# A four-layer decoder trunk with expert retrieval: wide weight pieces in the second layer, per-head waits, three value slots on VectorE while mixing, and a shorter second mixing

## The reference

```python
def peer(xn, w_q, sub_keys, u_tab, v_tab):
    q = (xt @ w_q).reshape(t, PEER_HEADS, 2, PEER_HALF)          # 8 heads
    s = einsum("thpd,hpnd->thpn", q, sub_keys)
    ...                                                           # top 16 of each half, top 16 of the 256 sums
    idx = take_along_axis(cand_idx, pos, axis=-1)                 # 128 experts per token
    g = softmax(top_s, axis=-1)
    ...
        u = take(u_tab, ic, axis=0)                               # (128 tokens, 8, 16, 1024)
        a = einsum("cd,chkd->chk", xc, u)
        w = gc * gelu(a)
        vv = take(v_tab, ic, axis=0)
        return einsum("chk,chkd->cd", w, vv)
```

## Time and profile before

| | |
|---|---|
| runs of the kernel | 1623.74, 1624.48, 1624.27 us; median 1624.27 us |
| profiled execution | 1625.22 us, of which the span of instructions is 1623.3 us |
| PE, DVE, ACT, POOL busy | 1339.6, 1073.2, 468.5, 1013.6 us |
| DMA | 617.13 MB, mean 380 GB/s |
| gathers (q0), weights and the rest (q1) | 536.94 MB, 79.26 MB |
| granted TensorE clock, mean | 0.91 |

### The profile page before, as it was taken

How to read it: one execution, slowest core, us unless ns; L and a number is a source line. 1 busy time by engine, 2 the same in 40 slices (tenths; PEclk the granted TensorE clock), 3 DMA queues, 4 the chain that set the end, 5 groups by cost and what they waited for, 6 DMA issues and landing times.

```text
span 1623.3 us, 17094 instructions
## 1 busy us (share of the span) xinstructions
PE 1339.6 (83%) x4558; PEld 769.0 (47%) x4558; DVE 1073.2 (66%) x2529; ACT 468.5 (29%) x1427; POOL 1013.6 (62%) x1099
## 2 busy tenths in 40 slices
PE   7999798888895899888777799989877978777775
PEld 7887544444552564354343376546444433322222
DVE  4248689988775545637787635664877977755555
ACT  0203333333332222432233221441333322211112
POOL 0006677777547655766666745675777677777774
PEclk9999999999997998899989899999988989888887
DMA  9519999999999999999999999999999999999997
GB/s 335 180 57 369 397 396 409 404 405 405 393 389 365 399 391 394 407 406 390 400 402 403 410 392 387 402 392 367 408 401 404 409 410 409 409 409 409 410 409 274
DMA packets 222153, 617.13 MB, mean 380 GB/s; under 512 B 18881, under 2 KB 88571, under 8 KB 222075
## 3 DMA queue, kind: packets, MB, share of 16 engines
q0 software_dynamic: 147456, 536.94, 84.0%
q1 hardware_dynamic: 74619, 79.26, 14.7%
HBM read 615.07 MB, written 1.05 MB: 380 GB/s over the span
## 4 chain that ended last, share of the span: by engine, by line
PE 33%; DMA 20%; POOL 15%; issue 13%; DVE 11%; ACT 6%; POOLq 0%; SPq 0%; DVEq 0%; ACTq 0%
DMA u_ring<-in_peer_u_dram,idx_now 18%; PE acc L807 16%; PE tile L777 13%; POOL v_ring L532 8%; POOL u_ring L532 7%; DVE u_ring L1022 5%; ACT diag L622 2%; ACT gelus L616 2%; DMA v_ring<-in_peer_v_dram,idx_now 2%; PE tile L909 1%; PE xf L777 1%; PE tile L904 1%; DVE xres L1049 0%; ACT pq L718 0%; PE tile L799 0%
## 5 line engine op out<-in xcount | busy, mean ns | idle before, releaser
L807 PE MATMUL acc<-v_ring,diag 128*128 128x512 f32 x1780 | 864.7, 644 | 117.7 <-ACT diag L622 64.8
L1022 DVE CUSTOM_DVE_ANT_0 u_ring<-u_ring,xf 128x1024 f32<-128x1024 f32 x512 | 613.5, 1215 | 275.3 <-DMA u_ring<-in_peer_u_dram,idx_now 273.0
L532 POOL DMA_INDIRECT v_ring<-in_peer_v_dram,idx_now x512 | 497.1, 971 | 291.8 <-PE acc L807 119.8
L807 PEld LDWEIGHTS acc<-v_ring,diag 128*128 128x128 f32 x1780 | 363.0, 209 | 589.3 <-issue 550.6
L532 POOL DMA_INDIRECT u_ring<-in_peer_u_dram,idx_now x512 | 501.2, 979 | 168.7 <-issue 138.9
L608 ACT ACTIVATE gelus<-dots 128x8 f32<-128x8 f32 x64 | 13.4, 209 | 526.4 <-DVE dots L1022 526.4
L622 ACT ACTIVATE diag<-ident,gelus 128x128 f32<-128x128 f32 x448 | 137.8, 388 | 2.1
L777 PE MATMUL tile<-w_ring,fT 128*128 128x256 f32 x480 | 110.3, 383 | 3.7 <-DVE fT L1171 3.7
L777 PEld LDWEIGHTS tile<-w_ring,fT 128*128 128x128 f32 x480 | 92.1, 193 | 27.4 <-issue 12.0
L616 ACT ACTIVATE gelus<-gelus,gates 128x1 f32<-128x1 f32 x512 | 102.1, 281 | 4.1 <-ACT gelus L608 2.3
L726 ACT ACTIVATE gexp<-best,gstat 128x16 f32<-128x16 f32 x32 | 9.8, 307 | 308.3 <-DVE best L1312 308.3
(11 more groups left out here) (170 smaller groups left out, 1046.1 us busy)
## 6 DMA issues: line engine op xcount, KB each, us to landing
w_ring<-in_peer_wq_dram SPq DMA_DIRECT2D x21, 1024.0 KB, 16.4
w_ring<-in_w_out_dram SPq DMA_DIRECT2D x12, 1024.0 KB, 24.0
w_ring<-in_w_kv_dram SPq DMA_DIRECT2D x12, 1024.0 KB, 16.5
u_ring<-in_peer_u_dram,idx_now POOLq DMA_INDIRECT x512, 10.7
v_ring<-in_peer_v_dram,idx_now POOLq DMA_INDIRECT x512, 10.6
w_ring<-in_w_in_b_dram SPq DMA_DIRECT2D x8, 1024.0 KB, 20.8
u_ring<-in_w_in_a_dram SPq DMA_DIRECT2D x4, 1024.0 KB, 12.2
w_ring<-in_w_mem_kv_dram SPq DMA_DIRECT2D x4, 1024.0 KB, 15.3
```

What stands on the lines that cost most here:

```text
L532: pool.indirect_dma_start(ring[:, s, :], None, rows_[:, :], bass.IndirectOffsetOnAxis(idx_now[:, column + s:column + s + 1], 0), element_o ...
L807: ins = pe.matmul(acc[:, 512 * n:512 * n + 512], diag[:, par * G + s, :], v_ring[:, s, 512 * n:512 * n + 512], start=(first and s == 0), s ...
L1022: dve.tensor_tensor_reduce(u_ring[:, s, :], u_ring[:, s, :], xf[:, :], 1.0, 0.0, ALU.mult, ALU.add, dots[:, par * G + s:par * G + s + 1])\
```

## The change

**Wide pieces.** `k`, `v`, `qf` of both chunks and the output projection of layer 1 are cut along the contraction: a piece is 256 rows by all 768 or 1024 columns, so that a partition gets two runs of 3 or 4 KB. PE takes such a weight with `by_depth`: it holds two PSUM tiles open and goes through the four pieces, two contraction blocks each. The first three pieces of each are given back by a semaphore of their own, `depth_used`. `out` of layer 1 becomes one step, `mix_out`, with two tiles of 512 columns.

**Own-head waits.** `heads_ready` asks in every phase only for the head whose indices come next.

**Three slots on VectorE.** In groups 0 to 10 of phases 1 and 2, slots 2, 5 and 7 are folded by DVE (`FOLDED_MIXING`), elsewhere slot 7 as before. The counters `v_added` and `v_folded` become one semaphore per slot, `slot_used`, on which POOL, ACT and DVE wait.

**Schedule.** The mixing of chunk 1 lies in groups 0 to 7 instead of 0 to 9. Head 5 joins `SHARED`. `mem_k`, `mem_v`, `keys` of layer 1 and some routing steps move. The last phase has side work in its first 4 groups instead of 6.

```diff
 FOLDED = [7]
+FOLDED_MIXING = [2, 5, 7]
...
+    ph, g = divmod(q, GROUPS)
+    return FOLDED_MIXING if 1 <= ph <= 2 and g <= 10 else FOLDED
...
-SHARED = [6, 7]
+SHARED = [5, 6, 7]
 ORDER_LAST = SHARED + [h for h in range(HEADS) if h not in SHARED]
-LAST_SIDES = 6
+LAST_SIDES = 4
...
-        side[0, (3, 5, 7, 9, 11, 12, 13, 14)[h]] += [("route", 1, h)]
+        side[0, (3, 5, 7, 9, 11, 12, 14, 15)[h]] += [("route", 1, h)]
...
-    side[0, 12] += [("mem_k", 1)]
-    side[0, 13] += [("mem_v", 1)]
-    side[0, 14] += [("keys", 1)]
+    side[0, 13] += [("mem_k", 1)]
+    side[1, 0] += [("mem_v", 1)]
+    side[1, 8] += [("keys", 1)]
...
+        else:
+            mix[1] += [("norm", c), ("k", c), ("v", c)]
+            mix[2] += [("forget", c), ("qf", c)] + attn(ph, 0)
+            mix[3] += attn(ph, 1, 2)
+            mix[4] += attn(ph, 3, 4, 5)
+            mix[5] += attn(ph, 6, 7, 8)
+            mix[6] += attn(ph, 9) + [("mix_out", ph), rms("ffn", ph)]
+            mix[7] += [("route", 2, 5), ("ffn", ph)]
+    for h in range(5):
         side[1, 9 + h] += [("route", 2, h)]
-    side[2, 8] += [("route", 2, 6)]
-    side[2, 10] += [("route", 2, 7)]
-    for g, h in zip((11, 12, 13, 14, 15), ORDER_LAST):
+    side[2, 9] += [("route", 2, 6)]
+    side[2, 11] += [("route", 2, 7)]
+    for g, h in zip((8, 10, 12, 13, 14, 15), ORDER_LAST):
         side[2, g] += [("route", 3, h)]
...
+            k = 2 * key[2]
+            return w.rearrange("(k p) n -> p k n", p=P)[:, k:k + 2, col:col + width]
...
-            return HEADS * (ph // 2) + (HEADS if ph == 1 else h + 1)
+            return HEADS * (ph // 2) + h + 1
...
-                    filled(sp, LAST_USE[PIECES[n - NW]])
+                    before = PIECES[n - NW]
+                    if before in DEPTH_USE:
+                        sp.wait_ge(depth_used, DEPTH_USE[before] + 1)
+                    else:
+                        filled(sp, LAST_USE[before])
...
-                if s in FOLDED:
-                    when(v_folded, GD * q + FOLDED.index(s) + 1 - GD)
-                else:
-                    when(v_added, GP * q + SUMMED.index(s) + 1 - GP)
+                when(slot_used[s], q)
...
+            def by_depth(tiles, src, ready=None):
+
+                outs = [take(key) for key in tiles]
+                keys, width = wide(tiles[0])[0:2]
+                deep = KD // len(keys)
+                for n, at in enumerate(keys):
+                    piece_landed(pe, at)
...
+                    for t, key in zip(outs, tiles):
...
+                        for k in range(n * deep, n * deep + deep):
+                            if moved:
+                                ins = pe.matmul(t[:, 0:count], src(k), w[:, k - n * deep, first:first + count],
+                                                start=(k == 0), stop=(k == KD - 1))
...
+                    if at in DEPTH_USE and LAST_USE[at] == tiles[-1]:
+                        ins.then_inc(depth_used, 1)
...
-                    if s in FOLDED and not (isinstance(q, int) and q == 0):
+                    if not (isinstance(q, int) and q == 0) and s in folded(q - 1):
                         fold(q - 1, 1 - par, (ph - 1 if q_first else ph) % 2, s)
```

More of the change, by code:

```diff
@@ L60, with folded, summed, sums_before @@
 FOLDED = [7]
+FOLDED_MIXING = [2, 5, 7]
 SUMMED = [s for s in range(G) if s not in FOLDED]
-GP, GD = len(SUMMED), len(FOLDED)
+def folded(q):
+    if not isinstance(q, int):
+        return FOLDED
+    ph, g = divmod(q, GROUPS)
+    return FOLDED_MIXING if 1 <= ph <= 2 and g <= 10 else FOLDED
+def summed(q):
+    return [s for s in range(G) if s not in folded(q)]
+def sums_before(q):
+    fixed = q if isinstance(q, int) else GROUPS * (PHASES - 1)
+    n = sum(len(summed(i)) for i in range(fixed))
+    return n if isinstance(q, int) else (q - fixed) * len(SUMMED) + n
 PE_LAST = G // 2
 ROUTE_PARTS = 2
-SHARED = [6, 7]
+SHARED = [5, 6, 7]
 ORDER_LAST = SHARED + [h for h in range(HEADS) if h not in SHARED]
-LAST_SIDES = 6
+LAST_SIDES = 4
 def place_of(ph, h):
@@ L155, with wide @@
 assert sorted(map(str, PE_START)) == sorted(map(str, START))
+def wide(tile):
+    kind = tile[0]
+    if kind == "k":
+        _, c, i = tile
+        return [("wk", c, n) for n in range(4)], CONV, 512 * i, (512, 256)[i], False
+    if kind == "v":
+        _, c, i = tile
+        return [("wv", c, n) for n in range(4)], CONV, CONV // 2 * i, CONV // 2, True
+    if kind == "qf":
+        _, c, i = tile
+        return [("wqf", c, n) for n in range(4)], D, 512 * i, 512, False
+    if kind == "out" and tile[1] >= 2:
+        _, ph, i = tile
+        return [("wout", ph, n) for n in range(4)], D, 512 * i, 512, True
+    return None
 def step_tiles(step):
@@ L176, in step_tiles @@
         return [("nT", step[1], i) for i in range(2)]
-    if kind in ("k", "v", "qf", "out"):
+    if kind in ("k", "v", "qf"):
+        return [(*step, i) for i in range(2)]
+    if kind == "out":
         return [step]
+    if kind == "mix_out":
+        return [("out", step[1], i) for i in range(2)]
     if kind == "forget":
@@ L800, in transposes, with group @@
                 done(ins)
-            def group(q, par, slots=SUMMED, first=False):
-                for s in slots:
-                    pe.wait_ge(diag_made, GP * q + SUMMED.index(s) + 1)
+            def group(q, par, slots=None, first=False):
+                made = sums_before(q) + 1
+                for s in slots or summed(q):
+                    pe.wait_ge(diag_made, made + summed(q).index(s))
                     pe.wait_ge(v_landed[s], 16 * q + 16)
@@ L1111, in start_norm @@
                         filled(dve, ("fT", ph - 2, 1))
-                    for i in range(4):
+                    for i in range(4 if ph < 2 else 2):
                         emptied(dve, ("out", ph, i))
```

158 lines of the change are left out of this document (100 added, 58 removed).

## The result

The changed kernel takes 1639.62 us (median of 6 runs, 1638.17 to 1641.33), the kernel before 1624.45 beside it (1623.74 to 1627.18): a ratio of 1.0091, 95% interval 1.0080 to 1.0102. The forecast was 1612. The profiled execution took 1640.53 us, its span 1638.5.

The account below looks back on a forecast made before the run. DMA was taken as the bound nearly throughout. From the profiled 1625.2 us, -11.9 - 3.0 - 3.5 + 6 = -12.4 gave 1612.8, less 0.95 for the median: 1612 us, range 1602 to 1622.

Parts of the forecast that it names:

- Wide pieces, -11.9: 28 weight pieces move in runs of 3 or 4 KB instead of 1 KB: -11.9 us, between 0 and -13.7.
- all of it is on the path, because DMA is full while these pieces arrive: Claim that the whole 11.9 us saved on wider weight pieces shortens the kernel.
- Rival 3: Run length of weight transfers costs nothing; only one load and the turn are saved: 1624 us, chance 0.06.
- One q piece less, -3.0: Phase 3 finds head 5 already loaded, saving DMA time: -3.0 us (2.6 to 3.0).
- Own-head wait, -3.5: End of phase 0: POOL's 16.05 us wait for indices goes; the DMA idle time alone is gained, -3.5 us.
- Three slots on VectorE and seven groups, +6 with the -3.0 apart: Mixing of both chunks: extra folds and chunk 1's fewer groups add 6 us, between -4.3 and +31.
- Chunk 0: I see no hole there now and count 0 to 3: Chunk 0 keeps nine groups and gets the same folds; no present DMA hole seen, 0 to 3 us added.
- the chain of chunk 1: From group 2's first dot to the ffn row: 156 us for five groups, DMA needing 147, about 9 idle.
- Rival 4: VectorE takes over in the mixing, folds lying in the dot-to-fetch loop: 1637 us, up to 1662 with POOL held; chance 0.09.
- The signs: If right: q1 packets about 53,100, no POOL wait at the first turn, mixing windows with weights nearer 410 GB/s.
- The hole of chunk 1: DMA idle expected between groups 3 and 6 of phase 2, with POOL waiting for dots or folds; about 9 us.
- The sign for wrong: Weight windows of 3 or 4 KB at 350 GB/s, or many mixing groups below share 1.0, PE idling, DVE not.

## Why the prediction was wrong, step by step

The forecast was 1612 us in a range of 1602 to 1622, measured were 1639.6. Three of its terms failed: wide pieces gave 7.1 us less than forecast, own-head waits 3.2 less, and folds with seven groups cost 16.5 more, 26.8 of the 27.6 us together.

- **Wide pieces, -11.9.** The size of the saving in DMA work was right: some 14 us by packet time, and packets fell to 53,163 where 53,100 were forecast. The step that failed is "all of it is on the path, because DMA is full while these pieces arrive". It counted bytes and not when they arrive: the same pieces as cover for the attention had a worth that I did not price. 4.8 us came through. The missing 7.1 belong to the eight pieces of `w_out`, which were priced at -3.6 and measured +3.9; the other 20 gave 8.7 for 8.3, all of it on the path. Rival 3 (run length costs nothing) is not borne out: those 14 us, and 600 to 620 us runs at 408 GB/s with weights under way where before had 396, both at full engines (1.03 and 1.04). The Trainium skill's page "DMA: Bandwidth & Descriptors" (Specifications) gives 512 B as the least transfer for line rate. These rates contradict it once more.
- **One q piece less, -3.0.** It is contained in seven groups and was not measured by itself.
- **Own-head wait, -3.5.** Measured -0.3 (-2.1 to +1.1). The step "what that gives is the DMA idle time alone" took a closed hole for a gain. The wait went as announced, and the time did not fall; where it went is open.
- **Three slots on VectorE and seven groups, +6 with the -3.0 apart.** Measured together 19.5 + 3.0 = 22.5, so 16.5 more. Two steps of it failed. "Chunk 0: I see no hole there now and count 0 to 3" laid chunk 0 under weights that are no longer there; 625 to 645 and 650 to 700 us lose 9.4 by rate, the first with one fold as well (300 GB/s in nine groups), the second with three alone, by the hold on POOL. And the chain of chunk 1 gave 9 us of idle for 156 us of groups, as one sum over five groups: it let DMA work of any of these groups fill time of any other. The trace shows that eight slots of each kind don't carry that far. POOL stopped for 16.73 us behind PE's merged steps and later for DVE, so a group loses by itself when its own chain is longer than 20.46 us. The terms of PE's chain were near (`k` 13.45 for 13.1, sums 8.75 for 8.7, `qf` 17.27 for 14.45).
- **Rival 4, 0.09.** Its price, 1637, was nearly the result, but by two causes of which it named one: the folds alone cost 11.5. It was put at 9% because PE's 3.5 us less per group seemed more than DVE's 2.56. In the group shown DVE took 1.53 more, just the 1.5 from which it decides, but the four rounds above go by the second half of this rival, POOL held at the folds: 3.2 and 1.1 us in chunk 0, 2.9 and 2.4 in chunk 1. The sum had measured that hold, 1.05 us for one fetch, and gave it no term in the +6.
- **The signs.** Right: packets and bytes of q1, no wait at the first turn, 407 GB/s there, weight windows near 410. The hole of chunk 1 began at 970 us, in group 2, a group earlier than forecast, with POOL waiting for PE's sums, not for dots or folds. The sign for wrong, shares below 1.0 over many mixing groups while PE idles and DVE does not, is what 650 to 700 us shows: 0.98, PE 34.6 of 50 us, DVE 38.4, POOL without a wait above 0.31 us.

## What to carry to other kernels

A transfer's saved time is worth what its stretch lacks: before counting it, ask what the transfer covered and whether it will now land in front of something that is waited for. Idle time must be reckoned per group, with as much run-ahead as the buffers hold, since a sum over several groups lets them lend each other time that they can't. Work may be moved from one engine to another where the first is the chain, group by group, and not over a whole phase by its mean; and what the moved work holds up on a third engine belongs in the sum.

## What the runs showed of the hardware

- Two DMA queues that both have work get packets through in about equal number (820 and 820 from 600 to 615 us with 4 KB on both; 1158 and 1301 with 1 KB on one), so the length of its packets sets a queue's share: 1.17 of 5.9 MB with 1 KB, 3.14 of 6.13 MB with 4 KB. A queue that has little to send leaves its turn to the other (158 and 1275 from 605 to 610 us).
- More bytes per second made the kernel slower: `w_out` in runs of 1 KB gave 1616.25 us in the median (one run of four 1620.14), in runs of 4 KB 1620.15, the step that uses them cut to match and nothing else changed.
- A fold of two SBUF inputs beside POOL's fetches lengthened those of u rows from 937 to 1094 ns in the mean of 650 to 700 us (20 and 18 fetches). A fetch that began during a fold ended some 0.8 us after it: folds of 666.61, 679.17 and 683.79 us end at 667.88, 680.45 and 685.07, the fetches that began in them at 668.69, 681.26 and 685.88. The Trainium skill's page "SBUF — State Buffer" (Who interferes with whom) infers that a tensor_tensor with both inputs in SBUF leaves descriptor writing alone. By these rows a two-input fold lengthens the fetch as a whole; which part of the fetch waits, no run shows.
